# Copies, roundings, a scaling and a value moved at four stage ends, and the border to the up projection written in another order, in a long fp32 kernel on one core

## The chip, the cores and the metric

The kernel runs on one core of one Trainium2 chip. The metric is the device time of one execution in microseconds (us). TensorE, the matmul engine, is PE in the rows; VectorE is DVE, ScalarE is ACT, GpSimd is POOL, and SP is the queue that issues most transfers.

## The reference, cut to what matters

The program is a forward pass over 1024 rows of width 1024 (and 256 rows of context): a first block of two layers (mLSTM heads with a pooling branch, then windowed attention), and a second block (gated linear attention beside differential attention, then a feed-forward part with a short convolution, then a gated addition of a small table). The part in which most of the change lies is the feed-forward part:

```
def conv_ffn(h, w_up, conv_w, conv_b, w_down):
    T = h.shape[1]
    u = h @ w_up
    up = jnp.pad(u, ((0, 0), (CONV_W - 1, 0), (0, 0)))
    c = conv_b + sum(up[:, j:j + T] * conv_w[j] for j in range(CONV_W))
    gate, val = jnp.split(c, 2, axis=-1)
    return (jax.nn.gelu(gate) * val) @ w_down
```

Here h is 1024 x 1024, `w_up` 1024 x 5632 and `w_down` 2816 x 1024. Between the blocks of a layer stand products with an output matrix, a norm of their rows, and the residual sum. Everything is in fp32.

## The kernel before, in words

**Splitting.** A product of fp32 operands is made of three matmuls on operands that are rounded to a shorter fp32 form: each operand is split into a high part, which a ScalarE copy rounds, and a low part, which VectorE gets by subtracting the high part from the operand; high by high, low by high and high by low are summed in one PSUM bank. So each weight tile, once landed, needs one pass of ScalarE and one of VectorE before TensorE can use it. For the weights of the earlier stages these are `split_hi` (L393) and `split_lo` (L402), for the turned rows `act_hi` (L633) and `vec_lo` (L640). `vec_scale` (L596) scales eight rows by their norm, TensorE turns them through the identity (L648), and `act_x` or `vec_value` (L618) reads them out of PSUM.

**Stages and borders.** The stages follow each other on TensorE without a break in the program: heads, pool, out0, in1, window attention, out1, the mixer of the second block, out2, up, down and the last part. The order of work on each engine is written out by hand, engine by engine: each engine has a program of its own with loops over steps `s`, and semaphores tie them together. An engine takes its instructions strictly in that order. A "border" is the stretch in which the last steps of one stage and the first of the next are mixed.

**Heads' end.** `copy_turned_y` (L1134) copies a turned tile of the last head out of PSUM; `oz_gates` (L1270 to L1273) makes a gate of four chained ScalarE passes, which VectorE multiplies in at L1430. TensorE's next transposes (L1125) write to the bank that the copies read; the pool stage begins with the matmuls at L2232.

**out0's and out1's end.** At out0's end ScalarE and VectorE split the first weights of in1 (`("aq", 0, 0)` and `("aq", 0, 1)`) among the last rows; TensorE's first matmul of in1 is L1673. `rows_part` is the common code of out1 and out2; with `following` it also splits the first weights of the next stage.

**Up.** The up projection takes 22 column tiles j (`NJ`), each with a tile of gate weights and a tile of value weights. Each pair is multiplied by a scheme of 7 products of quarter size (Strassen-Winograd), 12 matmuls each, all at L4365. For it VectorE makes four sums of the weights (`up_sums`, L4221 to L4226); ScalarE rounds gate tile (`up_gate_hi`, L4233), last quarter (`up_last_hi`, L4247) and the sums (`up_sum_hi`, L4261); VectorE makes the low parts (`up_gate_lo` L4239, `up_last_lo` L4252, `up_sum_lo` L4268). The products come out through ScalarE (`read_p1` L4488 or L4484, `read_p5` L4499, `read_u2` L4503, `read_c21` L4507) and VectorE (`c11` L4602, `c12` L4607, `c22` L4613), then through the convolution and the gelu: `gate_first` L4514, convolution of the gate L4616 and L4618, `square` L4520, `gelu_arg` L4627, `sigmoid` (four chained passes, L4524 to L4527), `gated` L4631, `value_first` L4532, convolution of the value L4616 and L4618 again, `product` L4640. The rows need terms of their own for the scheme (`up_term1` to `up_term4`, L4278 to L4296, and their low parts `term_lo`, L4596), made at the border. The weights have three raw buffers, and a load waits until the low part that last used its buffer is made:

```
def up_load(K, sp, n):              # n = 2j for the gate tile, 2j + 1 for the value tile
    if n >= 3:
        old, value = divmod(n - 3, 2)
        sp.wait_ge(K.s_l22 if value else K.s_la, old + 1)    # up_last_lo(old) or up_gate_lo(old)
        sp.wait_ge(K.s_sum, 4 * old + 4)
    ...
    sp.dma_start(K.up_raw[:, n % 3, :]...).then_inc(K.up_in[n % 3], 16)
```

So the gate tile of j = 3 is loaded when `up_last_lo(1)` is done, and that of j = 4 when `up_last_lo(2)` is done. `up_gate_hi(3)` stands in ScalarE's order at j = 1, in front of `square(0)`, `read_p1(1)` and `sigmoid(0)`; `up_gate_hi(4)` at j = 2.

**Down.** The down projection has 42 steps; a step loads rows of the up projection's result, which were stored to memory (L4345), and weights (L4842), sums them (L4965, L4966), splits them (`high` L4949 and L4955, `low` L4984 and L4987) and multiplies at L4924, where TensorE waits for the lows of step s. `down_hi(s)` and `down_lo(s)` are the first steps' `high` and `low`, placed in up's last tile.

## Time and profile before

| | |
|---|---|
| time, median of 3 runs | 3210.89 us (3208.25 to 3211.14) |
| time of the profiled execution | 3210.22 us |
| span of the profiled execution | 3208.4 us |
| mean granted TensorE clock | 0.994 |
| PE busy | 3130.8 us, 98% of the span |
| VectorE, ScalarE, GpSimd busy | 62%, 51%, 3% |

A row of the timeline shows when an instruction started, how long it took, and in brackets how long its engine had been idle ahead of it and what ended that. Neighbouring instructions overlap by some 0.1 us in these records, so the time that an instruction takes from its engine's stream is read from start to start: 1.13 for a pass of 1.22, 0.60 for one of 0.68.

### The profile page before, as it was taken

How to read it: one execution, taken by the hardware profiler on the slowest of the kernel's cores; microseconds unless marked ns; L12 is line 12 of the kernel's file. 1: busy time of each engine (PE TensorE's matmuls, PEld its weight loads, DVE VectorE, ACT ScalarE, POOL GpSimd, SP SyncE). 2: the span in 40 equal slices, each digit the busy share in tenths (PEclk: the TensorE clock that was granted, in tenths of full speed). 3: DMA queues.
4: the chain of work that ended last, by engine and by line, in shares of the span. 5: the costliest groups of instructions: out<-in, count | busy, mean ns of one | idle time of the engine just before them, and what ended most of it. 6: DMA issues, size and time to landing. Idle time of an engine off the chain costs nothing. (4 is left out here: it accounts for less than half of the span.)

```text
span 3208.4 us, 43173 instructions
## 1 busy us (share of the span) xinstructions
PE 3130.8 (98%) x17124; PEld 2568.1 (80%) x17124; DVE 1983.5 (62%) x3094; ACT 1634.9 (51%) x2679; POOL 111.8 (3%) x244
## 2 busy tenths in 40 slices
PE   7999999999999999999999999998998999999998
PEld 5988889898888888888787777886686888878886
DVE  7544444445445688732688463446849888878765
ACT  5352443534433447414688453425736777765455
POOL 2000000000000000001000000000000000000000
PEclk9999999999999999999999999999999999999999
DMA  6202011020442567213400541110052222235664
GB/s 216 71 5 86 30 57 60 32 70 15 154 140 96 196 205 258 93 27 88 109 2 2 136 141 53 29 57 27 1 207 88 79 79 86 86 140 182 235 231 150
DMA packets 204921, 322.05 MB, mean 100 GB/s; under 512 B 29339, under 2 KB 117248, under 8 KB 204720
## 3 DMA queue, kind: packets, MB, share of 16 engines
q1 hardware_dynamic: 182800, 241.37, 23.4%
q0 software_dynamic: 20848, 77.85, 7.0%
q8 instruction: 136, 2.23, 0.3%
q14 instruction: 65, 0.53, 0.1%
q10 hardware_dynamic: 1072, 0.07, 0.0%
HBM read 271.97 MB, written 47.28 MB: 100 GB/s over the span
## 5 line engine op out<-in xcount | busy, mean ns | idle before, releaser
L402 DVE TENSOR_TENSOR W_rounded<-W,W_rounded 128x2048 fp32r<-128x2048 f32 (+2 forms) x119 | 201.8, 1696 | 279.3 <-ACT W_rounded L393 275.8
L393 ACT ACTIVATE W_rounded<-W 128x2048 fp32r<-128x2048 f32 (+1 forms) x107 | 168.2, 1572 | 213.6 <-DMA W<-in_ab_w_in 60.0
L4924 PE MATMUL G<-down_ring_rounded 128*128 128x512 f32 x924 | 213.5, 392 | 1.9 <-DVE down_ring_rounded L4987 1.8
L1172 PE MATMUL G<-W_rounded,HT_rounded 128*128 128x512 f32 x640 | 213.7, 415 | 0.0
L2232 PE MATMUL G<-HT_rounded,W_rounded 128*128 128x512 f32 (+1 forms) x768 | 207.8, 355 | 0.0
L1216 PE MATMUL G<-HT_rounded,W_rounded 128*128 128x512 f32 (+1 forms) x768 | 206.6, 355 | 1.0 <-PEq L667 1.0
L4924 PEld LDWEIGHTS G<-down_ring_rounded 128*128 128x128 f32 x924 | 174.1, 189 | 39.4 <-DVE down_ring_rounded L4987 2.8
L3472 PE MATMUL G<-W_rounded,HT_rounded 128*128 128x512 f32 x640 | 201.2, 395 | 0.0
L2232 PEld LDWEIGHTS G<-HT_rounded,W_rounded 128*128 128x128 f32 x768 | 136.5, 188 | 24.8 <-issue 3.5
L1216 PEld LDWEIGHTS G<-HT_rounded,W_rounded 128*128 128x128 f32 x768 | 135.8, 188 | 22.5 <-issue 1.2
L1407 DVE SCALAR_TENSOR_TENSOR c_state<-c_state,decay_all,CC 128x514 f32<-128x514 f32 x64 | 48.0, 750 | 156.9 <-PE CC L1201 156.9
L3472 PEld LDWEIGHTS G<-W_rounded,HT_rounded 128*128 128x128 f32 x640 | 118.5, 188 | 28.2 <-issue 2.0
L1172 PEld LDWEIGHTS G<-W_rounded,HT_rounded 128*128 128x128 f32 x640 | 120.1, 188 | 25.1
L1216 PE MATMUL G<-HT_lo,W_rounded 128*128 128x512 f32 (+1 forms) x384 | 136.4, 355 | 0.0
L2232 PE MATMUL G<-HT_lo,W_rounded 128*128 128x512 f32 (+1 forms) x384 | 136.4, 355 | 0.0
L2994 PE MATMUL G<-out_ring_rounded 128*128 128x512 f32 x576 | 132.0, 390 | 1.3 <-DVE out_ring_rounded L3076 1.3
L1673 PE MATMUL G<-W_rounded,HT_rounded 128*128 128x512 f32 x416 | 130.1, 393 | 1.1 <-DVE W_rounded L402 1.1
L2994 PEld LDWEIGHTS G<-out_ring_rounded 128*128 128x128 f32 x576 | 107.8, 188 | 24.6 <-DVE out_ring_rounded L3076 2.1
L3472 PE MATMUL G<-W_rounded,o_turned_lo 128*128 128x512 f32 x320 | 126.9, 397 | 0.0
L1977 ACT ACTIVATE HT<-HT,neg_max 128x641 f32<-128x641 f32 (+1 forms) x128 | 102.1, 798 | 46.1 <-DVE neg_max L1996 43.5
L1172 PE MATMUL G<-W_rounded,HT_lo 128*128 128x512 f32 x320 | 125.5, 392 | 0.0
L1996 DVE CUSTOM_DVE_ANT_0 HT<-PS,win_masks,neg_sink 128x640 f32<-128x640 f32 (+1 forms) x128 | 103.8, 848 | 31.6 <-PE PS L1911 31.3
...
## 6 DMA issues: line engine op xcount, KB each, us to landing
...
```

Source lines behind the costliest of these rows:

```text
L393: ins = a.activation(self.half(key, True)[:, at], self.half(key, False, False)[:, at], ACT.Copy)
L402: ins = v.tensor_tensor(self.half(key, False)[:, at], self.half(key, False, False)[:, at], self.half(key, True)[:, at].bitcast(F32), ALU.s ...
L1172: ins = pe.matmul(G[:, K.par(key), :], x[y][:, 4 * kh + k, r * P:(r + 1) * P], wv[z][:, k, :], start=(kh == 0 and k == 0 and (y, z) == SPL ...
L1216: ins = pe.matmul(G[:, K.par(key), 0:n], wv[y][:, k, cc], x[z][:, k, c0:c0 + n], start=(k == 0 and (y, z) == SPLIT_PASSES[0]), stop=(k == ...
L1407: v.scalar_tensor_tensor(out=cs[:, d, :, :], in0=cs[:, d, :, :], scalar=dec[:, d, h, c:c + 1], in1=prod, op0=ALU.mult, op1=ALU.add).then_i ...
L1673: ins = pe.matmul(bank(key), x[y][:, 4 * kh + k, r * P:(r + 1) * P], w[z][:, k, :], start=(kh == 0 and k == 0 and (y, z) == SPLIT_PASSES[0 ...
L1977: a.activation(probs(u, b)[:, c0 * P:641], probs(u, b)[:, c0 * P:641], ACT.Exp, scale=-1.0, bias=nm[:, j % 32:j % 32 + 1], accum_out=sm[:, ...
L1996: v.tensor_tensor_reduce(probs(u, b)[:, c0 * P:640], PS[:, blk(at + c0, 5 - c0)], msk[:, which, c0 * P:640], -0.125, sink[:, hd:hd + 1], A ...
L2232: ins = pe.matmul(bank(key, n), w[y][:, k, cc], x[z][:, k, c0:c0 + n], start=(k == 0 and (y, z) == SPLIT_PASSES[0]), stop=(k == KT - 1 and ...
L2994: ins = pe.matmul(G[:, bank[r], :], x[y][:, m, r * P:(r + 1) * P], w[z][:, m, :], start=(p in (P1, P5) and q == 0 and m == 0 and (y, z) == ...
L3472: ins = pe.matmul(bank(key), x[y][:, 4 * kh + k, r * P:(r + 1) * P], w[z][:, k, :], start=first, stop=last)
L4924: ins = pe.matmul(G[:, bank[r], :], x[y][:, m, r * P:(r + 1) * P], w[z][:, m, :], start=(p in (P1, P5) and q == 0 and m == 0 and (y, z) == ...
```

## The change

At the end of the last head, two copies of turned rows stand in front of the gate's four passes instead of behind them. At out0's end the two first weight splits of in1 move one place forward on ScalarE and on VectorE. At out1's end the last turned value and the scaling stand ahead of the weight split. At the border to the up projection, `up_last_lo(0)` and the row terms 3 and 4 move back, `up_gate_lo(2)` forward, and the first three tiles have an order of their own on VectorE and ScalarE. At the border to the down projection, step 3's high and low parts are made inside up's last tile, ahead of `value_first(21)` and of the convolution of the value; the down loops start at step 4. The number of instructions of each engine stays as it is, and the orders of TensorE, SP and GpSimd are the same.

```
@@ -1342,11 +1342,11 @@
                     norm(h, ends_at[s])
-                if s >= 16 and h + 1 < H and s - TURN_AFTER in ends_at:
+                if s >= (16 if h + 1 < H else 17) and s - TURN_AFTER in ends_at:
                     copy_turned_y(a, h, ends_at[s - TURN_AFTER])
...
                     oz_gates(h, gated_at[s])
-                if (s < 16 or h + 1 == H) and s - TURN_AFTER in ends_at:
+                if s < (16 if h + 1 < H else 17) and s - TURN_AFTER in ends_at:
                     copy_turned_y(a, h, ends_at[s - TURN_AFTER])
@@ -2657,13 +2657,15 @@
             if s == len(steps) - 1 and following:
+                for r in due(s, 1):
+                    B.act_x(a, ch, r)
                 K.split_hi(a, following[0])
...
             for r in last[:1 if gated else len(last)] if s == len(steps) else last[1:] if s == len(steps) + 1 and gated \
-                    else due(s, 1) if s < len(steps) else []:
+                    else due(s, 1) if s < len(steps) - int(bool(following)) else []:
                 B.act_x(a, ch, r)
@@ -2722,18 +2724,24 @@
             if s == len(steps) - 1 and following:
+                for r in due(s, 2, 1):
+                    B.vec_value(v, r, TR[:, :], *turned(r))
+                for r in due(s, 1):
+                    B.vec_scale(v, r)
                 K.split_lo(v, following[0])
...
                 tail[2](v, s)
-            for r in due(s, 1) if s < len(steps) else last[1:] if s == len(steps) + 1 else \
+            if s == len(steps) + 1 and tail is not None:
+                tail[3](v)
+            for r in due(s, 1) if s < len(steps) - int(bool(following)) else last[1:] if s == len(steps) + 1 else \
                     last[:1] if s == len(steps) and not gated else []:
...
                 K.split_lo(v, following[2])
-            for r in due(s, 2, int(split)):
+            for r in due(s, 2, int(split)) if s != len(steps) - 1 or not following else []:
                 if split and r not in defer and not (tail is not None and s == len(steps)):
@@ -3193,10 +3201,10 @@
         scaled(a, ch, 6)
+        K.split_hi(a, ("aq", 0, 0))
         B.act_hi(a, 5)
-        K.split_hi(a, ("aq", 0, 0))
+        K.split_hi(a, ("aq", 0, 1))
         scaled(a, ch, 7)
-        K.split_hi(a, ("aq", 0, 1))
         B.act_hi(a, 6)
@@ -3251,11 +3259,11 @@
         value(v, 5)
+        K.split_lo(v, ("aq", 0, 0))
         B.vec_lo(v, 5)
         gate(v, 7)
-        K.split_lo(v, ("aq", 0, 0))
+        K.split_lo(v, ("aq", 0, 1))
         value(v, 6)
-        K.split_lo(v, ("aq", 0, 1))
         B.vec_lo(v, 6)
@@ -4123,18 +4131,17 @@
             up_term1(K, v, 0)
-            up_last_lo(K, v, 0)
-        elif s == 13:
+        elif s == 14:
             up_gate_lo(K, v, 1)
             up_term2(K, v, 0)
-            up_term3(K, v, 0)
-        else:
-            up_term4(K, v, 0)
+
+    def between_lo(v):
+        up_last_lo(K, v, 0)
 
...
                      parts=split_at, n_parts=4, ahead=0, presplit=[("out2", 0, 0), ("out2", 0, 1)],
-                     prev=diff, tail=(load_first, first_hi, first_lo))
+                     prev=diff, tail=(load_first, first_hi, first_lo, between_lo))
     K.up_rows_done = rows.finished
@@ -4544,8 +4551,8 @@
             term_hi(n, half)
+        read_p5(0)
         up_sum_hi(K, a, 1, 0)
-        read_p5(0)
         read_u2(0)
@@ -4557,19 +4564,28 @@
                 K.down_hi(a, 0)
+            if j == 2:
+                read_p1(j)
             square(j - 1)
-            if j < 3:
+            if j == 1:
                 read_p1(j)
...
             read_p5(j)
+            if j == 1:
+                read_c21(j - 1)
+                read_u2(j)
             sigmoid(j - 1)
-            read_c21(j - 1)
-            read_u2(j)
+            if j == 1:
+                up_sum_hi(K, a, j + 1, 0)
+            else:
+                read_c21(j - 1)
+                read_u2(j)
             value_first(j - 1)
...
                 up_last_hi(K, a, j + 1)
-                up_sum_hi(K, a, j + 1, 0)
+                if j > 1:
+                    up_sum_hi(K, a, j + 1, 0)
                 up_sum_hi(K, a, j + 1, 1)
@@ -4579,6 +4595,7 @@
         read_c21(NJ - 1)
+        K.down_hi(a, 3)
         value_first(NJ - 1)
@@ -4639,12 +4656,14 @@
 
+        up_term3(K, v, 0)
+        up_term4(K, v, 0)
         rows.values(v, 8)
         up_term1(K, v, 1)
+        up_gate_lo(K, v, 2)
         up_term2(K, v, 1)
...
             term_lo(n, half)
-        up_gate_lo(K, v, 2)
         up_sum_lo(K, v, 0, 0)
@@ -4653,19 +4672,21 @@
         up_sum_lo(K, v, 0, 1)
-        up_sums(K, v, 1)
         for n, half in LOWS[6:8]:
             term_lo(n, half)
+        up_sums(K, v, 1)
         c11(0)
-        up_last_lo(K, v, 1)
+        up_sum_lo(K, v, 1, 0)
         c12(0)
-        up_sum_lo(K, v, 1, 0)
         for n, half in LOWS[8:10]:
             term_lo(n, half)
+        c22(0)
+        up_last_lo(K, v, 1)
         for j in range(1, NJ):
...
                 v.wait_ge(s_ready, 1)
-            c22(j - 1)
+            if j > 2:
+                c22(j - 1)
             gate_conv(j - 1)
@@ -4673,8 +4694,15 @@
                 K.down_lo(v, 0)
+            if j == 1:
+                up_gate_lo(K, v, j + 2)
             gated(j - 1)
-            if j + 2 < NJ:
+            if j == 1:
+                up_sum_lo(K, v, j + 1, 0)
+                c11(j)
+                c12(j)
+                c22(j)
+            elif j + 2 < NJ:
                 up_gate_lo(K, v, j + 2)
@@ -4684,9 +4712,9 @@
             product(j - 1)
-            if j < 3:
+            if j == 2:
                 c11(j)
-            if j + 1 < NJ:
+            if 2 <= j < NJ - 1:
                 c12(j)
@@ -4694,6 +4722,7 @@
         gated(NJ - 1)
+        K.down_lo(v, 3)
         value_conv(NJ - 1)
@@ -5002,7 +5031,7 @@
 
-        for s in range(3, 40):
+        for s in range(4, 40):
             high(a, s)
...
...
```

**ScalarE at the end of the heads.** L1270 to L1273 are the gate's passes, L1134 the copies, L1278 the next square. Before:

```order
L478 ACTIVATE head_ss<-head_ss,eps 128x1
L479 ACTIVATE head_ss<-head_ss 128x1
L1270 ACTIVATE qk_conv<-G,cut 128x512
L1271 ACTIVATE qk_conv<-qk_conv,cut 128x512
L1272 ACTIVATE qk_conv<-qk_conv,one 128x512
L1273 ACTIVATE qk_conv<-qk_conv 128x512
L1134 ACTIVATE qk_conv<-X,cols 128x128 x2
L1278 ACTIVATE qk_conv,head_ss<-h_rows 128x256
```

and now:

```order
L478 ACTIVATE head_ss<-head_ss,eps 128x1
L479 ACTIVATE head_ss<-head_ss 128x1
L1134 ACTIVATE qk_conv<-X,cols 128x128 x2
L1270 ACTIVATE qk_conv<-G,cut 128x512
L1271 ACTIVATE qk_conv<-qk_conv,cut 128x512
L1272 ACTIVATE qk_conv<-qk_conv,one 128x512
L1273 ACTIVATE qk_conv<-qk_conv 128x512
L1278 ACTIVATE qk_conv,head_ss<-h_rows 128x256
```

The copies go ahead of the whole gate. On VectorE and TensorE nothing changes here.

**VectorE at the border to up, tile 0's last products.** The names are those of the weights' sums (L4268 their low parts), the rows' low parts (L4596), c11 (L4602), c12 (L4607), c22 (L4613) and `up_last_lo(1)` (L4252). Before:

```order
L4268 TENSOR_TENSOR up_sum430_rounded_17906<-up_sum430_exact_17905,up_sum43_hi0_rounded_17910 128x1024
L4221 TENSOR_TENSOR up_sum121_exact_17899<-up_w_in_17883 128x512
L4222 TENSOR_TENSOR up_sum431_exact_17907<-up_w_in_17883 128x512
L4224 TENSOR_TENSOR up_sum121_exact_17899<-up_sum121_exact_17899,up_w_in_17883 128x512
L4226 TENSOR_TENSOR up_sum431_exact_17907<-up_w_in_17883,up_sum121_exact_17899 128x512
L4596 TENSOR_TENSOR up_rows_rounded_17878<-up_rows_exact_17877,up_t3_hi_17886 128x4x256 x2
L4602 TENSOR_TENSOR W_1<-G_124,W_1 128x512
L4252 TENSOR_TENSOR up_last1_rounded_17916<-up_w_in_17883,up_last1_rounded_17916 128x512
L4607 TENSOR_TENSOR W_1<-G_124,W_1 128x512
L4268 TENSOR_TENSOR up_sum121_rounded_17900<-up_sum121_exact_17899,up_sum12_hi1_rounded_17904 128x1024
L4596 TENSOR_TENSOR up_rows_rounded_17878<-up_rows_exact_17877,up_t4_hi_17888 128x4x256 x2
L4613 TENSOR_TENSOR up_value0_17917<-G_124,up_value0_17917 128x512
```

and now, where each line number is 7 or 17 higher:

```order
L4275 TENSOR_TENSOR up_sum430_rounded_17906<-up_sum430_exact_17905,up_sum43_hi0_rounded_17910 128x1024
L4613 TENSOR_TENSOR up_rows_rounded_17878<-up_rows_exact_17877,up_t3_hi_17886 128x4x256 x2
L4228 TENSOR_TENSOR up_sum121_exact_17899<-up_w_in_17883 128x512
L4229 TENSOR_TENSOR up_sum431_exact_17907<-up_w_in_17883 128x512
L4231 TENSOR_TENSOR up_sum121_exact_17899<-up_sum121_exact_17899,up_w_in_17883 128x512
L4233 TENSOR_TENSOR up_sum431_exact_17907<-up_w_in_17883,up_sum121_exact_17899 128x512
L4619 TENSOR_TENSOR W_1<-G_124,W_1 128x512
L4275 TENSOR_TENSOR up_sum121_rounded_17900<-up_sum121_exact_17899,up_sum12_hi1_rounded_17904 128x1024
L4624 TENSOR_TENSOR W_1<-G_124,W_1 128x512
L4613 TENSOR_TENSOR up_rows_rounded_17878<-up_rows_exact_17877,up_t4_hi_17888 128x4x256 x2
L4630 TENSOR_TENSOR up_value0_17917<-G_124,up_value0_17917 128x512
L4259 TENSOR_TENSOR up_last1_rounded_17916<-up_w_in_17883,up_last1_rounded_17916 128x512
```

`up_last_lo(1)`, with whose end the load of the gate tile of j = 3 begins, goes from behind c11 to behind c22: a low part of the sums, c12, two row lows and c22 now stand ahead of it.

**VectorE at the border to down, the end of the last tile.** `gated` is L4631, the convolution L4616 and L4618, `product` L4640, step 3's lows L4984 and L4987 into `down_ring_rounded6`. Before:

```order
L4631 TENSOR_TENSOR W_1<-W_1 128x1024
L4616 SCALAR_TENSOR_TENSOR W_1<-up_value1_17918,cols_4,W_1 128x1023
L4618 SCALAR_TENSOR_TENSOR W_1<-up_value1_17918,cols_4,W_1 128x1022
L4640 TENSOR_TENSOR up_value1_17918<-W_1 128x1024
L4984 TENSOR_TENSOR down_ring_rounded6_17935<-down_ring6_17927,down_ring_rounded6_17935 128x1024
L4987 TENSOR_TENSOR down_ring_rounded6_17935<-down_right_sum_17939,down_ring_rounded6_17935 128x1024
```

and now, with higher line numbers (L5013 and L5016 for the lows):

```order
L4648 TENSOR_TENSOR W_1<-W_1 128x1024
L5013 TENSOR_TENSOR down_ring_rounded6_17935<-down_ring6_17927,down_ring_rounded6_17935 128x1024
L5016 TENSOR_TENSOR down_ring_rounded6_17935<-down_right_sum_17939,down_ring_rounded6_17935 128x1024
L4633 SCALAR_TENSOR_TENSOR W_1<-up_value1_17918,cols_4,W_1 128x1023
L4635 SCALAR_TENSOR_TENSOR W_1<-up_value1_17918,cols_4,W_1 128x1022
L4657 TENSOR_TENSOR up_value1_17918<-W_1 128x1024
```

The two lows stand ahead of the convolution and the product, which are all that the last rows' store waits for.

## Rows read from the trace of the kernel before

**Rows 1.** The page: busy time, share, instructions.

```profile
PE 3130.8 (98%) x17124; PEld 2568.1 (80%) x17124; DVE 1983.5 (62%) x3094; ACT 1634.9 (51%) x2679; POOL 111.8 (3%) x244
```

**Rows 2.** Timeline of ACT at the heads' end: start, duration, instruction.

```profile
814.55 0.61 ACT L1134 ACTIVATE qk_conv<-X,cols 128x128 f32<-128x128 f32 x2
```

**Rows 3.** Timeline of DVE there; in brackets idle time before, and releaser.

```profile
814.67 0.42 DVE L1430 TENSOR_TENSOR qk_conv<-G,qk_conv 128x256 f32<-128x256 f32 x1 [0.26 <-ACT qk_conv L1273]
```

**Rows 4.** Timeline of PE there.

```profile
815.21 0.44 PE L1125 MATMUL X<-ident,h_rows 128*128 128x128 f32 x2 [1.24 <-ACT qk_conv L1134]
815.42 0.47 PE L2232 MATMUL G<-HT_rounded,W_rounded 128*128 128x512 f32 x1
```

**Rows 5.** Timeline of DVE at out0's end.

```profile
1291.32 1.23 DVE L640 TENSOR_TENSOR HT_lo<-out_spare,HT_rounded 128x1024 fp32r<-128x1024 f32 x1 [1.12 <-ACT HT_rounded L633]
...
1294.92 2.29 DVE L402 TENSOR_TENSOR W_rounded<-W,W_rounded 128x2048 fp32r<-128x2048 f32 x1
```

**Rows 6.** Timeline of PE there.

```profile
1297.26 0.50 PE L1673 MATMUL G<-W_rounded,HT_rounded 128*128 128x512 f32 x1 [1.15 <-DVE W_rounded L402]
```

**Rows 7.** Timeline of DVE at out1's end.

```profile
1879.37 2.29 DVE L402 TENSOR_TENSOR W_rounded<-W,W_rounded 128x2048 fp32r<-128x2048 f32 x1 [2.93 <-ACT W_rounded L393]
...
1882.25 1.21 DVE L618 TENSOR_TENSOR r_h_turned<-TR,cols 128x1024 f32<-128x1024 f32 x1
```

**Rows 8.** Timeline of PE there.

```profile
1883.61 0.63 PE L648 MATMUL TR<-ident,r_xs 128*128 128x128 f32 x4 [1.58 <-DVE r_h_turned L618]
```

**Rows 9.** Stretches: length, busy time and instructions per engine, PE clock, DMA share, GB/s.

```profile
2414.00:2476.00 62.00, 52.18 (x224) 40.39 (x224) 58.82 (x62) 35.63 (x44) 1.07 (x2) 0.99 0.24 77
2474.20:2878.00 403.80, 403.54 (x1728) 325.19 (x1727) 338.68 (x348) 291.09 (x333) 0.00 (x0) 1.00 0.27 87
2474.54:2477.95 3.41, 3.41 (x9) 2.67 (x8) 3.38 (x4) 1.85 (x2) 0.00 (x0) 0.50 0.08 29
2477.95:2481.30 3.35, 3.35 (x16) 2.69 (x15) 3.31 (x6) 3.32 (x6) 0.00 (x0) 1.00 0.00 0
2880.73:2884.14 3.41, 3.41 (x9) 2.64 (x8) 1.44 (x2) 0.00 (x0) 0.00 (x0) 0.50 1.03 354
```

**Rows 10.** Timeline of DVE at the border to up.

```profile
2449.35 0.68 DVE L4252 TENSOR_TENSOR up_last_rounded<-up_w_in,up_last_rounded 128x512 fp32r<-128x512 f32 x1
...
2469.78 0.69 DVE L4252 TENSOR_TENSOR up_last_rounded<-up_w_in,up_last_rounded 128x512 fp32r<-128x512 f32 x1
...
2492.01 1.21 DVE L4268 TENSOR_TENSOR up_sum_rounded<-up_sum_exact,up_sum_hi_rounded 128x1024 fp32r<-128x1024 f32 x1
```

**Rows 11.** Timeline of ACT there.

```profile
2453.90 1.06 ACT L4233 ACTIVATE up_gate_hi_rounded<-up_w_in 128x1024 fp32r<-128x1024 f32 x1 [1.24 <-DMA up_w_in<-in_w_up]
...
2460.22 1.16 ACT L4524 ACTIVATE W<-W,cut 128x1024 f32<-128x1024 f32 x1 [0.32 <-DVE W L4627]
...
2474.47 1.06 ACT L4233 ACTIVATE up_gate_hi_rounded<-up_w_in 128x1024 fp32r<-128x1024 f32 x1 [0.33 <-DMA up_w_in<-in_w_up]
...
2479.52 1.15 ACT L4524 ACTIVATE W<-W,cut 128x1024 f32<-128x1024 f32 x1
```

**Rows 12.** Timeline of PE: product 6 of tile 1.

```profile
2459.47 0.51 PE L4365 MATMUL G<-up_t_hi,up_sum_hi_rounded 128*128 128x512 f32 x1 [0.52 <-ACT W L4488]
```

**Rows 13.** Timeline of PE: product 6 of tile 3.

```profile
2495.18 0.40 PE L4365 MATMUL G<-up_t_hi,up_sum_hi_rounded 128*128 128x512 f32 x1
```

**Rows 14.** Waits of PE from 2878 us to the end: total, times, longest.

```profile
PE G L4924 <- DVE down_ring_rounded L4987: 1.8, 1, 1.8
```

**Rows 15.** The chain that ended last, at the border to down: start, us, what.

```profile
2872.49 1.25 ACT W L4532
2873.77 1.29 DVE W L4616
...
2879.37 6.82 DMA down_pairs<-in_w_down
...
2911.95 0.73 PE G L4924 x2
```

88 lines of the change are left out of this document (58 added, 30 removed).

## The prediction, as put on record

> **What bounds the kernel now.** The page first: TensorE is busy 3130.8 us of a span of 3208.4, 98% [rows 1], so only its idle 77.6 us can go, and an edit on another engine counts only where TensorE waits for it. The timelines then show the waits at the changed places: 1.24 us at the heads' end [rows 4], 1.15 at out0's end [rows 6], 1.58 at out1's end [rows 8]. At the border to up the stretches are the view: from 2414 to 2476 us TensorE is busy 52.18 of 62.00 us, 9.8 idle, while VectorE is busy 58.82; from 2474.20 to 2878.00 TensorE is busy 403.54 of 403.80, so the tiles behind the border have no wait to give [rows 9]. At the border to down there is one wait of 1.8 for VectorE's lows, and none after it that the table would name [rows 14]. Last the granted clock: it is 0.50 (the lower level, 1.2 GHz) from 2474.54 to 2477.95, right behind the border's last wait, and again from 2880.73 to 2884.14, behind the wait in down; 9 matmuls run in either, against 16 in the 3.35 us after the first [rows 9]. So a low stretch costs half of 3.41, 1.7 us.
>
> The sum is made against the profiled execution, whose time is 3210.22 for a span of 3208.4 and 0.7 below the median of 3210.89. A kernel of this length can be told from another by about 0.2%, 6.4 us: below 3204.5 is faster, above 3217.3 slower.
>
> **Heads' end: +0.25.** The two copies (0.61 for both in the row, 0.50 of ScalarE's stream [rows 2]) go ahead of four gate passes. TensorE's wait of 1.24 before its transposes goes [rows 4], but the last gate pass ends 0.50 later. VectorE's multiplication by the gate starts 0.26 after an idle time that this pass ended [rows 3]; it moves from 814.67 to 815.17 and ends at 815.59. Its operand is a PSUM bank that the pool's first matmul needs free. That matmul started at 815.42, pushed there by the transposes [rows 4]; now the bank holds it until some 815.67. The stall moves by one instruction and grows by 0.25. Bounds: if the bank is not what holds it, −1.24; if the gate's passes are slowed further, +0.5. I take +0.25.
>
> **out0's end: −1.15.** The split of in1's first weight takes 2.29 from 1294.92, and the matmul that waits for it starts at 1297.26 after 1.15 idle [rows 5, 6]. The split now goes ahead of the pass at 1291.32 (1.14 start to start) and of a gate of two passes that lasts up to the split; ScalarE's copy of it moves ahead likewise. It can start over 1.15 earlier, so the whole wait goes. What moves back is the low part of a row group and a gate, work of the stage that ends, whose next readers stand behind in1's first products. Bounds −1.3 and 0.
>
> **out1's end: −1.58.** TensorE waits 1.58 for the turned value at 1882.25, which stands behind the weight split of 2.29 [rows 7, 8]. Value and scaling now go first, in 2.93 us in which VectorE was idle waiting for ScalarE's copy [rows 7]; TensorE's transposes find their rows. The split then ends later, but its weights are wanted only after those transposes and the products behind them. Bounds −1.58 and −0.5.
>
> **Border to up: +3.2.** In the early part waits become shorter, since values, scalings and `up_gate_lo(2)` come sooner. That does not reach the end, because VectorE, ScalarE and the loads form a chain that now runs later, and TensorE must meet it at tile 3. Step by step, each shift against before:
> - `up_last_lo(1)` started at 2449.35 [rows 10]. Now a sum's low part (1.13), c12 (0.60), two row lows (2.27) and c22 (0.60) stand ahead: +4.6 or 4.7. Its end releases the load of the gate tile of j = 3. Before, it ended at 2449.95 and ScalarE's `up_gate_hi(3)` started at 2453.90 after 1.24 us of idle time that the transfer ended [rows 11], so a load takes 3.9 from there. Now `up_gate_hi(3)` starts at 2458.6 and ends at 2459.6.
> - `square(0)` and `read_p1(1)` (0.97 and 0.48) stand behind it on ScalarE: 2461.1. TensorE's product 6 of tile 1, which waited 0.52 for that read and started at 2459.47 [rows 12], starts at 2461.2.
> - `sigmoid(0)` started at 2460.22 [rows 11]. Now it is behind `read_u2(1)`, which needs product 6, 12 matmuls of 0.23 or 2.8 us: 2464.0, and 0.6 for the read and the handing over: 2464.7, +4.5. `gated(0)` shifts by as much.
> - Behind `gated(0)` now stand a sum's low part (1.13) and c11, c12, c22 (0.60 each), 2.9 in place of one pass of 1.1 ahead of the convolution: `up_last_lo(2)`, 2469.78 before [rows 10], shifts by 6.4. So does the load of j = 4, and `up_gate_hi(4)`, 2474.47 before with an idle 0.33 ended by the transfer [rows 11], starts at 2480.8.
> - Behind it stand `read_p1(2)` and `square(1)`, then the argument of the gelu and `sigmoid(1)`: 2480.8 + 0.97 + 0.5 + 0.97 + 1.2 + 0.2, 2484.6 against 2479.5 [rows 11], +5.1. `gated(1)` and all of VectorE's work behind it shift by 5.1, up to tile 3's first low part of the sums, 2492.01 before [rows 10], now 2497.1, ending at 2498.3.
> - Tile 3's product 6 takes it. Before, it started at 2495.18 without a wait, 2.0 after the low part was done [rows 10, 13]. Now it starts at about 2498.4.
>
> So TensorE leaves the border 3.2 later than before, with four waits of some 2 us (before products of tiles 0 or 1, twice; tile 2; tile 3) in place of those removed. Every shift here hangs on the load: if it landed 1.5 us sooner, the sum were 1.7; if other transfers slow it to 6, it is +5. Bounds: 0 and +6; below nothing only if the chain does not bind, which is a rival.
>
> **Border to down: +1.95.** The lows of step 3 (two passes of 1.13) move ahead of the convolution of the last value. It started at 2873.77, as soon as `value_first(21)` (2872.49, 1.25) was done [rows 15]. That now stands behind two ScalarE copies of the 1.06 us form, 0.95 each from start to start, so it is done 1.9 later; VectorE's lows lie in that time, and the convolution starts at 2875.7. From it runs a chain without slack: convolution, product, store, load of rows and weights at 2879.37 (6.82 us), sums, two more loads, lows, and the matmul at 2911.95 [rows 15]. All of it shifts by 1.95. The wait of 1.8 goes [rows 14], but the matmul at 2911.95 had waited 0.1 for its chain, so TensorE, early by 1.8, waits there for 1.8 plus 1.95. Bounds: −1.8 (if the loads catch up) and +2.5.
>
> **The clock: +1.7.** Before has two low stretches, each behind a wait of about 2 us in a place where others lie near. The new border has waits as long, one more of them late; I count one more low stretch, 1.7. The page "Perfetto Trace Analysis" of the Trainium skill, section Matmul Optimizations, says that TensorE scales with its utilization, so that matmuls should come back to back in batches; "TensorE: Matmul & The Clock Gate", on a second failure mode, tells of short pauses that make the clock go down and up. The trace agrees in part: from 2414 to 2476 us the mean clock is 0.99 in spite of 9.8 us of waits, and it fell behind the last of them alone [rows 9]. By these pages alone the four waits would cost up to 6.8.
>
> **Sum:** 3210.2 + 0.25 − 1.15 − 1.58 + 3.2 + 1.95 = 3212.9, and 1.7 for the clock: 3214.6.
>
> **The rivals.**
> - *The waits go and nothing comes back (chance 0.12).* Then 1.24 + 1.15 + 1.58 + 1.8 and most of the 9.8 at the border to up are gained, with two low stretches (3.4): down to 3191.3, and about 3199 if half of the border's idle time stays. It needs the gate tile of j = 3 to be loaded without delay, or the chain to have some 5 us of slack; VectorE's 58.82 busy of 62.00 [rows 9] speaks against it. "Perfetto Trace Analysis", section Optimization Strategy, has this as its rule: find the gaps on the most contended engine and let what blocks them start sooner. The edits do that for each gap alone.
> - *The first parts gain, up's chain is milder, the rest as above (0.23).* The load lands early enough or the waits end 2 to 3 us sooner, with no further low stretch: 3214.6 − 1.7 − 2.5, some 3210; with down hidden too, 3208.
> - *Up's chain holds TensorE longer and the clock falls more than once (0.25).* The mechanism is the same queue, `up_last_lo` to load to `up_gate_hi` to `read_p1`; each of the four waits of about 2 us may start a low stretch of 1.7, and while it lasts the reads that ScalarE waits for come later too. Two stretches more than forecast give 3218.0, three 3219.7. It decides from two on: above 3217.3.
> - *Forecast (0.40):* 3211 to 3217.3.
>
> **How the numbers follow.** Faster than 3204.5 happens in the first rival (0.12, of which 0.11 is below the bound). Slower than 3217.3 happens in the third, and in a tail of the forecast: 0.29. The rest, 0.60, is the same. The predicted time is that of the forecast. The range leaves out most of the first rival and the far tail of the third: 3205 to 3220.5; the forecast's own is 3211 to 3217.3.
>
> **What would show it.** Heads' end: the wait of 1.24 gone, one of about 1.5 before the pool's first matmul, for VectorE. out0 and out1: no wait at L1673, nor before the transposes at out1. Up: `up_gate_hi(3)` late by 4 to 5 us after a wait for the transfer, `up_gate_hi(4)` by about 6; waits of TensorE at product 6 of tiles 1, 2 and 3. Down: the wait of 1.8 gone, and one of 3 to 4 us at about 2912, for lows. The prediction is wrong if tile 3 starts without a wait, if the clock rows show no low stretch at the border, or if TensorE enters down earlier than its loads and still never waits.

## The result, and the profile after

The changed kernel takes 3216.03 us (median of 16 runs, 3212.26 to 3219.12) against 3209.32 for the kernel before (16 runs, 3207.17 to 3213.0). The ratio is 1.0019, 95% interval 1.0012 to 1.0026: it is slower by 6 us, the interval 4 to 8. The profiled execution has a span of 3212.4 us, a time of 3214.22 and a mean clock of 0.993.

The page's row for TensorE, against [rows 1]: 3.3 us more busy, 4.0 more span.

```profile
PE 3134.1 (98%) x17124; PEld 2570.7 (80%) x17124; DVE 1983.0 (62%) x3094; ACT 1634.8 (51%) x2679; POOL 112.4 (3%) x244
```

The waits of TensorE in the changed kernel, largest first of those that the change made or touched (total, times, longest). L4495 is `read_p1`, L4510 `read_u2`, L5016 the lows of down, L1430 VectorE's multiplication by the gate:

```profile
PE G L4372 <- ACT W L4495: 6.3, 2, 4.2
PE G L4953 <- DVE down_ring_rounded L5016: 4.6, 2, 2.5
...
PE G L4372 <- ACT W L4510: 2.9, 2, 2.7
...
PE TR L648 <- DVE r_xs L596: 1.7, 1, 1.7
PE G L2232 <- DVE qk_conv L1430: 1.6, 1, 1.6
```

The reader is to see what is not there: the 1.24 for the copies, 1.15 for in1's weights and 1.58 for the turned value [rows 4, 6, 8]; and what is new: 6.3 and 2.9 for reads that ScalarE makes, 4.6 for the lows of down in place of 1.8 [rows 14].

**Heads' end.** TensorE and then VectorE, answering to [rows 3, 4]:

```profile
813.73 0.38 PE L1125 MATMUL X<-ident,h_rows 128*128 128x128 f32 x2
815.68 0.47 PE L2232 MATMUL G<-HT_rounded,W_rounded 128*128 128x512 f32 x1 [1.57 <-DVE qk_conv L1430]
```

```profile
815.11 0.42 DVE L1430 TENSOR_TENSOR qk_conv<-G,qk_conv 128x256 f32<-128x256 f32 x1 [0.79 <-ACT qk_conv L1273]
```

The transposes run 1.48 earlier than before, and the pool's first matmul starts at 815.68 instead of 815.42, after 1.57 us for L1430 (0.33 more wait than the 1.24 before), which itself had waited 0.79 for the gate's last pass.

**out0's and out1's end.** TensorE at in1's first matmul, then at the transposes of out1, answering to [rows 6, 8]; neither row has a bracket, so neither waits:

```profile
1296.08 0.62 PE L1673 MATMUL G<-W_rounded,HT_rounded 128*128 128x512 f32 x2
```

```profile
1878.87 0.93 PE L648 MATMUL TR<-ident,r_xs 128*128 128x128 f32 x7
```

**Border to up.** VectorE, ScalarE and TensorE of the changed kernel, answering to [rows 10 to 13]:

```profile
2451.63 0.69 DVE L4630 TENSOR_TENSOR up_value<-G,up_value 128x512 f32<-128x512 f32 x1 [1.00 <-PE G L4372]
2452.24 0.68 DVE L4259 TENSOR_TENSOR up_last_rounded<-up_w_in,up_last_rounded 128x512 fp32r<-128x512 f32 x1
...
2474.21 0.69 DVE L4259 TENSOR_TENSOR up_last_rounded<-up_w_in,up_last_rounded 128x512 fp32r<-128x512 f32 x1
```

```profile
2456.73 1.06 ACT L4240 ACTIVATE up_gate_hi_rounded<-up_w_in 128x1024 fp32r<-128x1024 f32 x1 [7.04 <-DMA up_w_in<-in_w_up]
...
2462.38 0.60 ACT L4510 ACTIVATE W<-G 128x512 f32<-128x512 f32 x1 [2.18 <-PE G L4372]
2462.87 1.14 ACT L4531 ACTIVATE W<-W,cut 128x1024 f32<-128x1024 f32 x1
...
2478.94 1.06 ACT L4240 ACTIVATE up_gate_hi_rounded<-up_w_in 128x1024 fp32r<-128x1024 f32 x1 [6.54 <-DMA up_w_in<-in_w_up]
2479.90 0.58 ACT L4495 ACTIVATE W<-G 128x512 f32<-128x512 f32 x1
```

```profile
2447.02 0.47 PE L4372 MATMUL G<-up_t_hi,up_sum_hi_rounded 128*128 128x512 f32 x1 [2.67 <-ACT W L4510]
...
2459.27 0.50 PE L4372 MATMUL G<-up_t_hi,up_sum_hi_rounded 128*128 128x512 f32 x1 [2.11 <-ACT W L4495]
...
2480.53 0.50 PE L4372 MATMUL G<-up_t_hi,up_sum_hi_rounded 128*128 128x512 f32 x1 [4.19 <-ACT W L4495]
...
2496.49 0.50 PE L4372 MATMUL G<-up_t_hi,up_sum_hi_rounded 128*128 128x512 f32 x1 [0.19 <-DVE up_sum_rounded L4275]
```

Since the border is entered 2.64 us earlier than before (the transposes' predecessors end at 2416.45 and 2419.09, start less wait), 2.64 is to be added to each to see the shift. `up_last_lo(1)` at 2452.24 is 5.5 later, `up_gate_hi(3)` at 2456.73 is 5.5 later after 7.04 us of idle time for the transfer, `sigmoid(0)` at 2462.87 is 5.3 later, right behind `read_u2(1)`, which waited 2.18 for TensorE; `up_gate_hi(4)` at 2478.94 is 7.1 later, again after 6.54 us for a transfer, and the read behind it at 2479.90 is what TensorE waits 4.19 us for. Tile 3 starts with a wait of 0.19 only.

Stretches of the changed kernel at the lower clock, with one at full clock between them, in the columns of [rows 9]:

```profile
2447.50:2450.90 3.40, 3.40 (x9) 2.63 (x9) 3.12 (x4) 2.08 (x2) 0.00 (x0) 0.50 0.49 141
2481.60:2485.00 3.40, 3.40 (x10) 2.64 (x9) 3.37 (x5) 3.08 (x4) 0.00 (x0) 0.50 0.00 0
2898.00:2901.40 3.40, 3.35 (x8) 2.67 (x9) 3.14 (x3) 1.80 (x2) 0.00 (x0) 0.51 0.95 327
2450.90:2454.30 3.40, 3.40 (x16) 2.74 (x16) 2.64 (x4) 0.00 (x0) 0.00 (x0) 1.00 0.06 12
```

Two low stretches at the border, each behind a wait, where the kernel before had one; one in down, as before.

**Border to down.** The chain that ended last in the changed kernel, answering to [rows 15], and TensorE's first wait for it:

```profile
2869.06 4.91 DMA down_right_sum<-in_w_down
...
2877.45 1.21 DVE W L4633
...
2881.25 0.32 SPq L4352
...
2884.58 8.76 DMA down_pairs<-in_w_down
...
2898.05 17.07 PE G L4953 x67
```

```profile
2892.99 1.19 PE L4953 MATMUL G<-down_ring_rounded 128*128 128x512 f32 x4 [2.55 <-DVE down_ring_rounded L5016]
```

VectorE at the first of the two lows that were moved ahead:

```profile
2875.08 1.23 DVE L5013 TENSOR_TENSOR down_ring_rounded<-down_ring,down_ring_rounded 128x1024 fp32r<-128x1024 f32 x1 [0.44 <-ACT down_ring_rounded L4978]
```

### The profile page after: what moved, and what is told of

It is laid out like the page before. It is cut to its first block and busy times, and to the rows that moved or that the text cites. A ratio compares the mean times of both kernels' runs of the same rounds, so it can differ in the third digit from the quotient of the medians.

```text
span 3212.4 us, 43173 instructions
## 1 busy us (share of the span) xinstructions
PE 3134.1 (98%) x17124; PEld 2570.7 (80%) x17124; DVE 1983.0 (62%) x3094; ACT 1634.8 (51%) x2679; POOL 112.4 (3%) x244
## 5 line engine op out<-in xcount | busy, mean ns | idle before, releaser
L2232 PEld LDWEIGHTS G<-HT_rounded,W_rounded 128*128 128x128 f32 x768 | 136.5, 188 | 26.6 <-issue 5.2
```

The costliest lines, as they stand in the source:

```text
L2232: ins = pe.matmul(bank(key, n), w[y][:, k, cc], x[z][:, k, c0:c0 + n], start=(k == 0 and (y, z) == SPLIT_PASSES[0]), stop=(k == KT - 1 and ...
```

## The experiments

Each kernel was timed against the kernel before on the same chip, 11 runs of each kernel and 27 or 33 of the kernel before. The intervals reach some 2.8 us to either side, so a difference of 1 us cannot be told by the time: the local readings come from the traces, one per kernel, and the times say what the whole gives.

### The parts alone

**Heads' end alone:** the first hunk of the diff and nothing else.

```
-                if s >= 16 and h + 1 < H and s - TURN_AFTER in ends_at:
+                if s >= (16 if h + 1 < H else 17) and s - TURN_AFTER in ends_at:
                     copy_turned_y(a, h, ends_at[s - TURN_AFTER])
```

> The kernel before with the copies of the last head ahead of the gate, and nothing else. Theory (the wait moves to the next holder of a bank): the wait of 1.24 us before TensorE's transposes is gone, the pool's first matmul waits some 1.5 us for VectorE's multiplication by the gate and starts 0.25 later than before; the time is the same within the noise, +0.25. Rival (the wait is simply removed): the pool starts 1.2 us earlier and no new wait stands there, -1.2.

Measured: 3212.14 against 3209.77 us, ratio 1.0004 (0.9995 to 1.0013), so no difference that the time can tell. TensorE in its trace:

```profile
816.49 0.47 PE L2232 MATMUL G<-HT_rounded,W_rounded 128*128 128x512 f32 x1 [1.57 <-DVE qk_conv L1430]
```

The wait stands behind the transposes, in front of the pool's first matmul and for L1430, as in the changed kernel and as long. The wait is moved; a gain of 1.2 is excluded by this row, a loss of 0.25 is not told by the time.

**out0's and out1's end alone:** the hunks of `rows_part`, without the new member of `tail`, and of `out0_part`.

```
+                for r in due(s, 1):
+                    B.act_x(a, ch, r)
                 K.split_hi(a, following[0])
...
+                for r in due(s, 2, 1):
+                    B.vec_value(v, r, TR[:, :], *turned(r))
+                for r in due(s, 1):
+                    B.vec_scale(v, r)
                 K.split_lo(v, following[0])
...
+        K.split_lo(v, ("aq", 0, 0))
         B.vec_lo(v, 5)
         gate(v, 7)
-        K.split_lo(v, ("aq", 0, 0))
+        K.split_lo(v, ("aq", 0, 1))
```

> The kernel before with the parts at out0's and at out1's end, and nothing else. Theory: both waits (1.15 and 1.58 us) are gone and nothing takes their place up to the attention stages, so TensorE is 1.15 earlier at in1 and 2.7 earlier behind out1, and the time falls by about 2.7, more if a stretch at the lower clock goes with it. Rival (the gain is given back in the stages behind, whose waits on the softmax chain grow by as much): the earlier start is seen at in1 but is gone by 2414 us, 0.

> The output parts alone once more, on the same chip as the two runs before it: 2.7 to 3 us below the kernel before, the two early-half kernels within 1 us of it; rival as above, the early-half kernels 2 to 3 us below it.

Measured in two comparisons: 3206.94 against 3209.77, ratio 0.9991 (0.9982 to 0.9999), and 3206.07 against 3210.01, ratio 0.9989 (0.9980 to 0.9997): 2.9 and 3.5 us faster, the forecast of 2.7 in both intervals. The first trace at in1's first matmul and at out1's transposes:

```profile
1297.50 0.63 PE L1673 MATMUL G<-W_rounded,HT_rounded 128*128 128x512 f32 x2
```

```profile
1879.73 0.82 PE L648 MATMUL TR<-ident,r_xs 128*128 128x128 f32 x6
```

No bracket stands in either row. (The time of 1297.50 is no earlier than before because the pool already started later in this execution, at 816.70 against 815.42; from there it is 480.8 us instead of 481.8.) Counted from the pool's start, TensorE is 3.6 us earlier at the first transposes of the border to up in the first trace and 1.7 earlier in the second, the longest of its 11 executions (3211.09), with 6.8 us more of low clock on the way than the first. No new wait eats the gain: in the first trace, up to 2414 us, the one wait that the kernel before had not is 0.61 at 1504, and the kernels with the heads' end alone and with up alone have it too (0.51 and 0.81).

**Border to up alone:** the hunks of the tail, `up_gate_lo`, `up_sums`, `up_last_lo`, the reads and the loops over j.

```
+            if j == 1:
+                read_c21(j - 1)
+                read_u2(j)
             sigmoid(j - 1)
...
         c11(0)
-        up_last_lo(K, v, 1)
+        up_sum_lo(K, v, 1, 0)
         c12(0)
-        up_sum_lo(K, v, 1, 0)
         for n, half in LOWS[8:10]:
             term_lo(n, half)
+        c22(0)
+        up_last_lo(K, v, 1)
```

> The kernel before with the part at the border to the up projection alone. Theory (the loads of the gate tiles of j = 3 and 4 start 4.6 and 6.4 us later, and reads that TensorE needs stand behind their rounding on ScalarE): waits of 2 to 4 us at product 6 of tiles 1 and 2, TensorE at tile 3 later by 3.2 without the clock and by about 5 with one more stretch at 1.2 GHz; the time grows by 3 to 5. Rival (what the changed kernel lost came from its down border alone, and the early part of the border gains): the time falls or stays, -3 to 0.

Measured: 3216.8 against 3209.77, ratio 1.0023 (1.0014 to 1.0032), 7.4 us slower; the whole loss of the changed kernel, and more than the 3 to 5 expected, with 5 inside the interval. TensorE waits 2.65, 2.03 and 4.16 us where the changed kernel waits 2.67, 2.11 and 4.19, and its trace has more of the lower clock in this border than any other, 13.7 us:

```profile
2448.00:2451.40 3.40, 3.27 (x8) 2.62 (x9) 3.40 (x4) 2.69 (x3) 0.00 (x0) 0.50 0.53 154
2461.60:2465.00 3.40, 3.40 (x10) 2.65 (x9) 3.02 (x4) 0.32 (x1) 0.00 (x0) 0.51 0.03 9
2482.10:2488.90 6.80, 5.90 (x14) 4.64 (x15) 3.72 (x5) 6.41 (x9) 0.00 (x0) 0.50 0.01 2
```

The stretch from 2461.6 has no counterpart in the changed kernel. It lies in product 6 of tile 1, and the read behind it on ScalarE (`read_u2(1)`), with `sigmoid(0)` behind that, waits 3.49 us for TensorE instead of 2.18; VectorE's first low part for tile 3 is 1.3 later than in the changed kernel, counted from where the border begins.

**Border to down alone:** `K.down_hi(a, 3)` ahead of `value_first`, `K.down_lo(v, 3)` ahead of `value_conv`, loops from 4.

```
         read_c21(NJ - 1)
+        K.down_hi(a, 3)
         value_first(NJ - 1)
...
         gated(NJ - 1)
+        K.down_lo(v, 3)
         value_conv(NJ - 1)
```

> The kernel before with step 3's high and low parts of down ahead of the last value's convolution, and nothing else. Theory (store and loads of the last rows start 2.0 to 2.2 us later, in a chain without slack): the wait of 1.8 us is gone and one or two of together 4.5 us stand near 2900, the time grows by 2 to 2.7. Rival (the chain is hidden and the removed wait is a gain): no wait behind 2880 us, the time falls by 1.8.

Measured: 3212.26 against 3209.77, ratio 1.0006 (0.9997 to 1.0014), +1.9, which the interval does not part from nothing. The trace does: the wait of 1.8 is gone, and TensorE waits twice for the lows behind it.

```profile
2891.53 3.01 PE L4926 MATMUL G<-down_ring_rounded 128*128 128x512 f32 x12 [2.27 <-DVE down_ring_rounded L4989]
2896.60 1.79 PE L4926 MATMUL G<-down_ring_rounded 128*128 128x512 f32 x6 [2.05 <-DVE down_ring_rounded L4989]
```

From the last matmul that waits in up (2856.15) to the end of the span it takes 354.95 us; with the old order this distance is 352.5 in the kernel before, and 352.6, 353.1 and 352.1 in the three runs above. So, against the mean of these four, 352.6, it is +2.4 here and +2.5 in the changed kernel (355.1). Over all traces of this study the distance is 353.7 to 355.1 in the four kernels with the new down order (mean 354.4) and 352.1 to 353.9 in the eight with the old (mean 352.8): 1.6 us, the forecast of 1.95 between these.

The parts add up within their intervals: the four ratios, with the mean of the two for the outputs, give 1.0023 together, and the changed kernel has 1.0019 (1.0012 to 1.0026).

### What in the border to up costs

**The load earlier:** in the changed kernel, `up_last_lo(1)` back behind `c11(0)`.

```
         c11(0)
+        up_last_lo(K, v, 1)
         up_sum_lo(K, v, 1, 0)
...
         c22(0)
-        up_last_lo(K, v, 1)
```

> The changed kernel with up_last_lo(1) on VectorE back right behind c11(0), so that the load of the gate tile of j = 3 is issued some 4 us earlier. Theory (load, rounding, read of product 1 in one row): the rounding of the gate tile of j = 3 on ScalarE starts when the earlier load lands, the wait of 2.11 us at product 6 of tile 1 falls to about 1, TensorE is 1.4 us earlier at tile 3 than in the changed kernel, and the time is 1 to 2 us shorter. Rival (VectorE's amount of work alone sets the border's end, and the place of one pass of 0.6 us is nothing): the waits only change places, 0.

Measured: 3213.22 against 3209.86, ratio 1.0012 (1.0003 to 1.0021), where the changed kernel has 1.0019; the order of the two is as expected, but the intervals overlap. In the trace the wait of 2.11 at product 6 of tile 1 is gone altogether, where about 1 was expected, and the next stays:

```profile
2482.51 0.80 PE L4372 MATMUL G<-up_t_hi,up_sum_hi_rounded 128*128 128x512 f32 x1 [4.28 <-ACT W L4495]
```

**The reads out of the queue:** in the changed kernel, the rounding of the gate tile behind the reads, in the first two rounds.

```
             gate_first(j - 1)
-            if j + 2 < NJ:
+            if 2 < j and j + 2 < NJ:
                 up_gate_hi(K, a, j + 2)
...
             if j == 1:
                 read_c21(j - 1)
+            if j < 3:
+                up_gate_hi(K, a, j + 2)
+            if j == 1:
                 read_u2(j)
             sigmoid(j - 1)
```

> The changed kernel with the rounding of the gate tiles of j = 3 and 4 moved back on ScalarE, behind square and the reads of products 1 and 5, in the first two rounds of the loop; the loads stay as late as the change made them. Theory (the late loads hurt only because the reads stand behind the rounding that waits for them): the waits of 2.11 and 4.19 us at product 6 of tiles 1 and 2 fall to about 0.5 and 1.2, one of about 2.4 appears at tile 3 for the low part of its sums, and TensorE leaves the border 3 us earlier than in the changed kernel; time 3 us shorter, 4.7 if a stretch at 1.2 GHz goes too. Rival (the lateness of the load itself is the cost, or VectorE's work): less than 1 us.

Measured: 3212.34 against 3209.86, ratio 1.0008 (0.9999 to 1.0017), 3.5 us less than the changed kernel's ratio gives; here too the intervals overlap. The wait at tile 1 is gone, the one at tile 2 is 2.96 instead of 4.19, and 0.70 stands at tile 3, where 0.5, 1.2 and 2.4 were expected:

```profile
2478.45 0.50 PE L4372 MATMUL G<-up_t_hi,up_sum_hi_rounded 128*128 128x512 f32 x1 [2.96 <-ACT W L4495]
...
2494.93 0.50 PE L4372 MATMUL G<-up_t_hi,up_sum_hi_rounded 128*128 128x512 f32 x1 [0.70 <-DVE up_sum_rounded L4275]
```

What is left at tile 2 is no matter of this queue. ScalarE's read, with nothing for the load in front of it any more, had been idle for VectorE's convolution of the gate (L4638 in this kernel):

```profile
2477.80 0.60 ACT L4495 ACTIVATE W<-G 128x512 f32<-128x512 f32 x1 [6.24 <-DVE W L4638]
```

### Is there a gain in the border at all?

**A candidate:** the output parts, this queue order, and tile 3's first low part of the sums early; heads' end and down as before.

```
             elif j + 2 < NJ:
+                if j == 2:
+                    up_sum_lo(K, v, j + 1, 0)
                 up_gate_lo(K, v, j + 2)
```

> A candidate: the parts at out0's and out1's end, the up border of the changed kernel with the ScalarE order of the run before it and with tile 3's first low part of the sums made right behind the gate's product; the heads' end and the border to down as in the kernel before. Theory (parts add up): the two output parts give 2.7, the border to up costs nothing or gives up to 0.3, so about 3 us below the kernel before, 3207. Rival (the early waits that the up part removed are a gain once the queue is free): 3 to 5 us more, 3202 to 3204.

Measured: 3210.76 against 3209.86, ratio 1.0000 (0.9991 to 1.0009). It missed: about 3 us were expected, and the gain of the output parts is used up by the border, which is 439.4 us long where the old order takes 436.0 (table below). The low part that was made early for tile 3 left a wait at tile 4 that the traces of the kernel before, the changed kernel and the three with its up order above do not have:

```profile
2516.63 0.50 PE L4372 MATMUL G<-up_t_hi,up_sum_hi_rounded 128*128 128x512 f32 x1 [1.16 <-DVE up_sum_rounded L4275]
```

**The early half alone**, on top of the output parts; the late half as before.

```
+        up_term3(K, v, 0)
+        up_term4(K, v, 0)
         rows.values(v, 8)
         up_term1(K, v, 1)
+        up_gate_lo(K, v, 2)
         up_term2(K, v, 1)
         for n, half in LOWS[0:2]:
             term_lo(n, half)
-        up_gate_lo(K, v, 2)
```

> The kernel with the two output parts alone, plus only the early half of the up part: up_last_lo(0) and the row terms 3 and 4 later, up_gate_lo(2) earlier; everything from up_sums(1) on as in the kernel before. Theory (VectorE is the bound of the border, so a wait removed early comes back): the waits of 2.3, 1.4 and 1.7 us shrink to 1.7 and 0.5, and the wait of 1.05 us behind them grows to about 4.5; TensorE reaches tile 2 within 0.2 us of the kernel with the output parts alone, and the time is the same as its time. Rival (the early half is the good one and the late half the bad one): 2 to 3 us faster than the output parts alone.

Measured: 3211.05 against 3210.01, ratio 1.0005 (0.9996 to 1.0014). The waits:

```profile
2419.17 1.09 PE L648 MATMUL TR<-ident,r_xs 128*128 128x128 f32 x8 [1.77 <-DVE r_xs L596]
...
2429.88 0.47 PE L4372 MATMUL G<-up_first_hi,up_gate_hi_rounded 128*128 128x512 f32 x1 [0.34 <-DVE up_gate_lo_rounded L4246]
...
2445.75 0.77 PE L4372 MATMUL G<-up_b_hi,up_sum_hi_rounded 128*128 128x512 f32 x1 [4.45 <-ACT up_value L4506]
```

The output parts alone, in their second trace, over the same stretch:

```profile
2421.20 1.09 PE L648 MATMUL TR<-ident,r_xs 128*128 128x128 f32 x8 [2.40 <-DVE r_xs L596]
...
2426.49 1.06 PE L648 MATMUL TR<-ident,r_xs 128*128 128x128 f32 x8 [1.40 <-DVE up_rows_exact L618]
...
2434.89 0.47 PE L4371 MATMUL G<-up_first_hi,up_gate_hi_rounded 128*128 128x512 f32 x1 [1.73 <-DVE up_gate_lo_rounded L4245]
...
2447.35 0.47 PE L4371 MATMUL G<-up_b_hi,up_sum_hi_rounded 128*128 128x512 f32 x1 [1.04 <-ACT up_value L4505]
```

1.77 + 0.34 + 4.45 is 6.6 us, and so is 2.40 + 1.40 + 1.73 + 1.04: the removed waits are back in one. So far as expected; but the time is 5 us above the output parts alone (3206.07 in the same comparison), where the same time was expected, and TensorE comes to product 6 of tile 2 57.2 us after the border begins instead of 55.0, where at most 0.2 was expected. Its trace has three times the low clock of the other in the border, 10.2 us against 3.4.

```profile
2444.60:2451.40 6.80, 5.65 (x13) 4.46 (x14) 3.78 (x6) 2.96 (x5) 0.00 (x0) 0.50 0.53 154
2475.30:2478.70 3.40, 3.40 (x10) 2.65 (x9) 3.36 (x3) 2.06 (x3) 0.00 (x0) 0.50 0.06 23
```

**The reads ahead of the sum's rounding**, on top of this:

```
-        up_sum_hi(K, a, 1, 0)
         read_p5(0)
         read_u2(0)
+        up_sum_hi(K, a, 1, 0)
```

> The kernel of the run before it, with the reads of products 5 and of the second sum of tile 0 ahead of up_sum_hi(1, 0) on ScalarE. Theory: the wait of 4.5 us was for reads that stand behind up_sum_hi(1, 0), which waits for VectorE's up_sums(1); with them ahead it splits into waits of about 1.2 and 1.7, but the end of the border moves by no more than 0.7, the time by less than 1 us. Rival (the reads were the bound): 3 us faster than the run before it.

Measured: 3208.35 against 3210.01, ratio 0.9994 (0.9985 to 1.0002), 2.7 us below the run before it.

```profile
2442.66 0.47 PE L4372 MATMUL G<-up_b_hi,up_sum_hi_rounded 128*128 128x512 f32 x1 [1.02 <-DVE up_sum_rounded L4275]
...
2447.41 0.50 PE L4372 MATMUL G<-up_t_hi,up_sum_hi_rounded 128*128 128x512 f32 x1 [1.71 <-DVE up_rows_rounded L4603]
```

The wait of 4.45 is split into 1.02 and 1.71; all waits of the border together are 8.6 us instead of 9.8, and one low stretch of 3.4 is left. The time moved by what the rival said (3), where less than 1 was expected, and it is still 2.3 above the output parts alone (the intervals overlap). The reads themselves are probably not the reason: the border's length less half its low time changed by little, as the next table shows, and most of the change is in the clock.

### The border's length and the clock

The length is from the point where TensorE begins to wait for the first transposes (start less wait of the L648 row) to its one wait at the end of up (the row at about 2856); low time is the granted clock at 0.50 in the border.

| kernel | order of the border | length, us | low time, us | length less half the low time |
|---|---|---|---|---|
| before | old | 436.8 | 3.4 | 435.1 |
| heads' end alone | old | 435.3 | 3.4 | 433.6 |
| outputs alone | old | 435.6 | 3.4 | 433.9 |
| outputs again | old | 436.9 | 3.4 | 435.2 |
| down alone | old | 435.3 | 3.4 | 433.6 |
| changed | new | 440.9 | 6.8 | 437.5 |
| up alone | new | 442.9 | 13.7 | 436.1 |
| load earlier | new | 438.4 | 6.8 | 435.0 |
| queue | new | 438.0 | 6.8 | 434.6 |
| candidate | new | 439.4 | 6.8 | 436.0 |
| early half | early half new | 439.1 | 10.2 | 434.0 |
| early half, reads ahead | early half new | 436.0 | 3.4 | 434.3 |

The old order takes 436.0 on the mean of five, always with one low stretch; the changed kernel 440.9, with two. The last column takes half of each low stretch as lost. That is the most it can cost; where TensorE would have had to wait anyway it costs less, and in the changed kernel one of the two cost nothing (below).

These are single executions. Each run also has a mean granted clock of its own; one less that clock, times the run's time, is the time that the clock withheld, again the most that it can have cost. Means over all runs, against those of the kernel before in the same comparison; the changed kernel's comparison has no clocks for the kernel before, and its withheld time is to be held against the other comparisons' 21.2 to 21.5:

| kernel | runs | withheld, us | mean time against before, us |
|---|---|---|---|
| before (33, 27 and 27 runs) | | 21.2, 21.2, 21.5 | |
| heads' end alone | 11 | 22.5 | +1.5 |
| outputs alone, two comparisons | 11, 11 | 22.2, 22.2 | −2.7, −3.5 |
| down alone | 11 | 21.0 | +1.9 |
| changed | 16 | 26.3 | +6.3 |
| up alone | 11 | 25.2 | +7.3 |
| load earlier | 11 | 24.5 | +3.6 |
| queue | 11 | 24.8 | +2.6 |
| candidate | 11 | 22.5 | +0.4 |
| early half | 11 | 26.6 | +0.8 |
| early half, reads ahead | 11 | 22.2 | −2.0 |

The changed kernel is withheld 5 us more than the kernel before, three low stretches' worth, and the early half 4.4 more than the output parts alone, against which it is 4.3 slower.

The version that beats both kernels is the outputs alone: 0.9991 and 0.9989 of the kernel before, so about 9 us below the changed kernel.

## Why the prediction was right, point by point

The forecast was 3214.6, the measured median 3216.03. As a difference it fits less well: +3.7 was forecast against the median of before that was given (3210.89, of three runs), and the ratio gives +6.1, with 3.9 as its lower end. That the two times are only 1.4 apart is in part luck, since those three runs lay 1.6 above the median of sixteen, 3209.32. The direction and the mechanism are the forecast's own: the output parts gain, the two late borders lose more. In the profiled executions the span grew by 4.0, against 4.4 in the forecast's sum: −2.6 up to the border to up (forecast −2.5), +4.0 in it (+4.9), +2.6 from it to the end (+1.95).

- **Heads' end, +0.25.** Right in mechanism and near in size in the trace: 815.68 against 815.42, with a wait of 1.57 for one of 1.24. Shown by the part alone: the same wait stands there.
- **out0's and out1's end, −1.15 and −1.58.** Right: neither wait is left, and both together gave 2.9 and 3.5 us in time. The changed kernel was 4.76 us ahead at 2201, more than these 2.7. Most of the rest was not the change's: in window attention the low stretch behind the wait at 1784 was 3.4 us long instead of 6.8, and a wait of 1.11 was 0.17 there; the kernels that do not touch these stages show both forms too. The attention after it gave 2.1 back, with 6.8 us more of low clock. So that the border to up begins 2.64 earlier, close to the sum of the forecast, is in part chance.
- **Border to up, +3.2 and +1.7 for one more low stretch.** Right in the chain, wrong in how the sum is split. Against the trace that the forecast was made from, the border is 4.0 longer (440.9 and 436.8), and product 6 of tile 3 starts 80.04 us after the border begins instead of 76.09, 3.95 later. Of the steps, `up_last_lo(1)` moved by 5.5, not 4.7, because c22 ahead of it waited 1.00 for TensorE, which had itself waited 2.67 for a read that stands behind `up_sum_hi(1, 0)` (the read of the second sum of tile 0) and then ran its product in the low stretch from 2447.5. I had counted a wait there and followed neither it nor the clock to VectorE. At the full clock the 12 matmuls would have been done at about 2450.0, before VectorE was free for c22 at 2450.63 (an estimate from 0.23 us a matmul). So both loads came 0.7 to 0.8 later than forecast (5.5 and 7.1 against 4.7 and 6.4). The last step was wrong in place: I put waits of some 2 us at tile 2 and at tile 3 alike; it was 4.19 at tile 2 and 0.19 at tile 3, so that the sign named against the forecast, tile 3 without a wait, was only just missed.
- **The 1.7 was put on top of a start that does not depend on it.** The forecast has product 6 of tile 3 wait for VectorE's low part, and then adds a low stretch of TensorE. In the changed kernel, from `up_gate_hi(4)` to that low part no step of VectorE or ScalarE waits for TensorE; VectorE waits 1.78 and 2.15 for ScalarE and then runs through:

```profile
2487.37 1.23 DVE L4648 TENSOR_TENSOR W<-W 128x1024 f32<-128x1024 f32 x1 [2.15 <-ACT W L4534]
...
2495.22 1.21 DVE L4275 TENSOR_TENSOR up_sum_rounded<-up_sum_exact,up_sum_hi_rounded 128x1024 fp32r<-128x1024 f32 x1
```

The low part starts 5.85 later than before, counted from the border's beginning (5.1 was forecast). The low stretch from 2481.6 only made TensorE arrive 1.7 later at a point where it would else have waited 1.9 instead of 0.19 (an estimate from these rows), so it cost nothing there. Measured, then: 3.95 for the chain, some 0.8 of it by way of the first low stretch, and nothing for the second.
- **That the chain of late load, rounding and read is the cost** is shown by taking it apart. The changed kernel, the one with the load earlier and the one with the reads out of the queue all have 6.8 us of low clock in the border, at the same two waits, and in all three product 6 of tile 3 waits for VectorE's low part (0.19, 0.38 and 0.70). It starts 80.0, 77.6 and 77.2 us after the border begins, and the lengths fall by 2.5 and 2.9; the wait at tile 1 goes in both. The forecast for these two had been 1.4 and 3.0. Each is one trace, and the times of the two agree in direction but overlap with the changed kernel's.
- **Border to down, +1.95.** Right in mechanism: the last value's convolution starts at 2877.4 in the changed kernel, 2.2 later relative to the end of up, and the whole loss is 2.5 there, 2.4 in the part alone, and 1.6 over all traces. What I left out: step 3's own tile landed only at 2873.97 (2869.06 and 4.91), so the lows waited 0.44 for its rounding. The waits came at 2893 and 2898, where the chain runs through the second load (8.76 from 2884.58), not at 2912.
- **The clock.** One low stretch more was counted, and the profile has one more; all five traces of the new order have at least two in the border, all five of the old have one. But the profiled execution, at 3214.22, was a mild one: over the 16 runs the clock withheld 26.3 us, 5 more than before, where the sum had 1.7. This is the term that was mis-sized for the time. How much of the 5 is a loss the runs do not settle, since a stretch can fall where TensorE would wait anyway. Why a given wait starts one and another does not, the runs do not settle: the old order's single one began between 2419.6 and 2424.9 in three traces and behind the last wait, at 2474, in two.
- **Against the rule** of the page "Perfetto Trace Analysis" of the Trainium skill, section Optimization Strategy (find the gaps of the most contended engine, make what blocks them start sooner), which was the first rival: it held where the work moved had slack behind it (out0, out1), and failed at the other three, where the engine that does the moved work is itself on the chain that the next gap waits for. The early half alone shows it with 6.6 us of waits where the old order has 6.6.

The rival with several low stretches (above 3217.3) was met in its stretches, though not in its time, by the up part alone: 13.7 us of low clock in the border, in an execution of 3214.70. Five of the 16 runs of the changed kernel took more than 3217.3; their mean clocks are 0.990 to 0.992, against 0.993 for the two fastest. They have no traces, so which stretches they had is not known.
